# Two transformer blocks on one core: VectorE takes all four channel tiles of the short convolution, GpSimd none

## The chip, the cores and the metric

The kernel runs on one core of a Trainium2 chip, as one launch. The metric is the device time of one execution in microseconds. The difference between two kernels is told as the ratio of their times on the same chip.

## The reference

Two blocks of two layers each work on one sequence of 256 tokens with 2048 channels, all in float32. The change touches the convolution mixer of the first block's two layers. Both layers multiply x by `w_in` (2048 x 7168), cut the product into ten parts, run three mixers (convolution, gated recurrence "hgrn2", retention) on them, multiply by `w_out`, and end with a feed-forward part. The convolution mixer is:

```python
def conv_mixer(a_in, gate_in, w_dw, b_dw, ln_g, ln_b):      # 512 channels, width 31, causal
    u = a_in * jax.nn.sigmoid(gate_in)
    y = lax.conv_general_dilated(u, w_dw[:, None, :], window_strides=(1,),
                                 padding=[(CONV_WIDTH - 1, 0)],
                                 dimension_numbers=('NWC', 'WIO', 'NWC'),
                                 feature_group_count=D_CONV) + b_dw
    return jax.nn.silu(layer_norm(y, ln_g, ln_b))
```

Each channel has its own 31 weights: for 512 channels and 256 tokens, output t of a channel is the sum over 31 taps of weight times the input at t - 30 + tap, plus a bias. The second block (attention and a delta rule) is not touched.

## The kernel before

**Weights.** All large products stream their weights from memory in blocks of 256 rows by 512 columns. SyncE loads a block into one of eight buffers `raw`, ScalarE makes its high half `w_hi` (`act_split`, L229), VectorE the low half `w_lo` = raw - w_hi (`dve_split`, L236), each in four slots, and TensorE runs twelve matmuls per block (`pe_block`, L252 to L254: hi by hi, hi by lo, lo by hi, for two row tiles and two token tiles). Semaphores tie the steps: SyncE reloads a buffer when VectorE has done its split (`lo_ready`), ScalarE may convert block c + 4 when TensorE has finished block c (`block_done`), VectorE follows ScalarE (`hi_ready`), TensorE waits for `lo_ready` (L245). Eight blocks make a unit of 512 output columns, which ScalarE copies out of the accumulators (L344).

**Mixers beside the weights.** After the first two units (the convolution's columns), the remaining twelve units of `w_in` run interleaved with the mixers. Each engine's program is written out by hand with an object `Meanwhile`, called `run`: `run(n)` puts the engine's part of the next n blocks between two mixer steps, `upto(run, n)` goes on to block n. ScalarE's and VectorE's parts are four blocks ahead of TensorE's.

**The convolution.** Channels lie on partitions in four tiles of 128. TensorE turns weights (L858) and gated input (L864) after four blocks; VectorE copies them to `conv_w` and `conv_u` (L887, L889), the latter with 30 zero columns ahead. In `dve_conv` VectorE goes through 31 taps. For each tap it treats the first three tiles (`DVE_CONV` = 3), one instruction each: the first tap writes y = u * w + bias (L898), every other one y = u * w_tap + y on 128 x 256 elements (L901), after waiting (`conv_tap`) for the instruction that made the same tile's y at the tap before. Then comes one split, `run(1)`, and, after taps 22, 26 and 27, steps of the recurrence's forget gate (`dve_hgrn_gates`: L1088 and L1089 read the turned gate out of the accumulators; L1098; L1100; in layer 1 also L1103 to L1111). Each tap is thus paired with one weight block.

**GpSimd's tile.** The fourth tile is GpSimd's (`pool_conv`, L839 to L850). [...] It starts when the first VectorE tap has signalled. After it GpSimd's next work waits for `h_cum` from VectorE (L1048).

**What waits for the convolution.** TensorE turns the forget gate after block 26 (L937), then goes on to block 38 (42 in layer 1), waits for all VectorE taps and for GpSimd's last (L872, L873), and turns the result back (L876) for the layer norm. ScalarE, after 28 blocks, waits for L1089, and computes softplus and the like (L998 to L1006), one split among them, then goes on with splits; from L1008 it waits for L1100 (in layer 1 for L1111) before the exponential of L1010 or L1014.

These are the lines in which a tap is paired with a split:

```python
        run(1)
        dve_hgrn_gates(dve, k, l, tap)
```

Of the kernel before, what the change touches and what calls it, by code (L numbers as in the profile page):

```python
# [21 lines left out]
DEPTH = 2  # L22
# [4 lines left out]
CONV_C = 512  # L27
CONV_W = 31
# [619 lines left out]
LOG_LB_MAX = math.log(1 - 1e-6)  # L648
LOG_1M_LB_MIN = math.log(1e-6)
CONV_T = CONV_W - 1 + SEQ  # L650
DVE_CONV = CONV_C // P - 1
LATE = 4


# [8 lines left out]
def first_buffers(k):  # L663
    K = 1024
    w, t1, t2 = k.scratch, k.t1, k.t2
# [38 lines left out]
    k.r_mv = k.sb_small("r_mv", [P, TT * HEADS, 2])  # L704
    k.r_rstd = k.sb_small("r_rstd", [P, TT * HEADS])
    count = k.count
    k.conv_pool, = count("conv_pool")
    k.conv_pad, k.conv_gate, k.h_gate, k.h_qsilu, k.r_gate = count("conv_pad", "conv_gate", "h_gate", "h_qsilu", "r_gate")
    k.conv_weights, k.conv_gated, k.conv_turned, k.conv_back, k.conv_var = \
        count("conv_weights", "conv_gated", "conv_turned", "conv_back", "conv_var")  # L710
# [111 lines left out]
    a.activation(ca, ca, ACT.Silu).then_inc(*k.conv_done.up())  # L822


def pool_conv(pool, k):

    g = k.nc.gpsimd

    def step(ins):
        ins.then_inc(*k.pool_step.up())  # L830
        pool.wait_ge(*k.pool_step.now())

    def weight(n):
        return k.conv_w[:, DVE_CONV, n:n + 1].to_broadcast([P, SEQ])

    y = k.conv_y[:, DVE_CONV, :]
    pool.wait_ge(*k.conv_tap.next("pool"))
    k.conv_tap.next("pool", DVE_CONV * CONV_W - 1)
    step(g.tensor_tensor(y, k.conv_u[:, DVE_CONV, 0:SEQ], weight(0), ALU.mult))  # L839
    g.tensor_tensor(k.conv_work[:, 1, :], k.conv_u[:, DVE_CONV, 1:1 + SEQ], weight(1), ALU.mult)  # L840
    step(g.tensor_tensor(y, y, weight(CONV_W), ALU.add))
    for tap in range(1, CONV_W):

        if tap + 1 < CONV_W:
            g.tensor_tensor(k.conv_work[:, (tap + 1) % 2, :], k.conv_u[:, DVE_CONV, tap + 1:tap + 1 + SEQ], weight(tap + 1),  # L845
                            ALU.mult)
        last = g.tensor_tensor(y, y, k.conv_work[:, tap % 2, :], ALU.add)
        if tap + 1 < CONV_W:
            step(last)
    last.then_inc(*k.conv_pool.up())  # L850


def pe_conv(pe, k, l, run):

    run(4)
    pe.wait_ge(*k.conv_rows_in.next("pe", 32))
    for c in range(4):
        last = k.nc.tensor.transpose(k.ps[:, 0, c * 32:(c + 1) * 32], k.conv_rows[:, c * P:(c + 1) * P],  # L858
                                     k.ident[0:CONV_W + 1, 0:CONV_W + 1])
    last.then_inc(*k.conv_weights.up())  # L860
    pe.wait_ge(*k.conv_gated.next("pe"))
    for c in range(4):
        for t in range(TT):
            last = k.nc.tensor.transpose(k.ps[:, 1 + c // 2, (c % 2) * SEQ + t * P:(c % 2) * SEQ + (t + 1) * P],  # L864
                                         k.proj[:, t, CA + c * P:CA + (c + 1) * P], k.ident)
    last.then_inc(*k.conv_turned.up())
    run(22)
    pe.wait_ge(*k.conv_tap.next("pe", 1))
    pe_hgrn_gates(pe, k, l, run)
    upto(run, 38 + LATE * l)  # L870
    pe.wait_ge(*k.h_kx.next("pe"))
    pe.wait_ge(*k.conv_tap.next("pe", DVE_CONV * CONV_W - 1))  # L872
    pe.wait_ge(*k.conv_pool.next("pe"))  # L873
    for t in range(TT):
        for c in range(4):
            last = k.nc.tensor.transpose(k.ps[:, 1 + t, c * P:(c + 1) * P], k.conv_y[:, c, t * P:(t + 1) * P], k.ident)  # L876
    last.then_inc(*k.conv_back.up())


def dve_conv(dve, k, l, run):  # L880
# [11 lines left out]
    dve.wait_ge(*k.dve_step.now())  # L892
    sem, done = k.conv_tap.now()
    for tap in range(CONV_W):
        for c in range(DVE_CONV):
            u, y = k.conv_u[:, c, tap:tap + SEQ], k.conv_y[:, c, :]
            if tap == 0:
                ins = v.tensor_scalar(y, u, k.conv_w[:, c, 0:1], k.conv_w[:, c, CONV_W:CONV_W + 1], ALU.mult, ALU.add)  # L898
            else:
                dve.wait_ge(sem, done + DVE_CONV * (tap - 1) + c + 1)  # L900
                ins = v.scalar_tensor_tensor(y, u, k.conv_w[:, c, tap:tap + 1], y, ALU.mult, ALU.add)  # L901
            ins.then_inc(*k.conv_tap.up())
        run(1)
        dve_hgrn_gates(dve, k, l, tap)
# [5 lines left out]
    for t in range(TT):  # L910
        last = v.bn_aggr(k.conv_mv[:, t, :], k.conv_stats[:, t, :])
# [483 lines left out]
def second_buffers(k):  # L1395
    K = 1024
    w, t1 = k.scratch, k.t1
# [80 lines left out]
    count, later = k.count, k.later  # L1478
# [17 lines left out]
    k.at_y, k.dn_wT, k.dn_w_kept, k.dn_turned, k.dn_turn_kept = \  # L1496
        later(DEPTH, k.r_roped, k.r_rope_free, k.r_qT, k.r_q, k.r_kT)
    k.dn_tap, k.dn_silu, k.dn_squared = later(DEPTH, k.r_k, k.r_o, k.r_var)
    k.dn_summed, = later(DEPTH * DVE_CONV * CONV_W, k.conv_tap)
    k.dn_rooted, k.dn_scaled, k.dn_qkT = later(DEPTH * (LEVELS + 1), k.h_rel, k.h_decay, k.h_factors)  # L1500
    k.dn_qkT_kept, k.dn_abs = later(DEPTH * (LEVELS + 2), k.h_scores, k.h_score_kept)
    k.dn_soft, k.dn_lnb = later(DEPTH * HEADS, k.r_scores, k.r_kept)
# [1312 lines left out]
def two_blocks_kernel(nc, dram, out):  # L2815
    k = set_up(nc, dram, out)
# [4 lines left out]
    with nc.Block() as block:  # L2821
# [26 lines left out]
        def _(pool):  # L2848
# [6 lines left out]
            for l in range(DEPTH):  # L2855
                if l:
                    pool.wait_ge(*k.turned.next("pool", BLOCKS))
                pool_first_rows(pool, k, l)
                pool_conv(pool, k)
                pool_hgrn(pool, k)  # L2860
                pool_retention(pool, k, l)

# [171 lines left out]
```

## Time and profile before

| | |
|---|---|
| Median of the timed runs | 3781.74 us (three runs, 3781.71 to 3783.3) |
| Profiled execution, span from first to last instruction | 3784.1 us |
| TensorE matmuls busy | 3541.0 us (94%) |
| VectorE busy | 2168.7 us (57%) |
| ScalarE busy | 1618.5 us (43%) |
| GpSimd busy | 419.4 us (11%) |
| TensorE's mean granted clock | 0.968 of full |
| L901 (taps on VectorE) | 180 instructions, 112.5 us |
| L845 (products on GpSimd) | 58 instructions, 62.4 us |

No time of the profiled execution other than its span is given; the page of the profile describes that one execution, which is 2.4 us longer than the median of the timed runs. Shares of busy time are means over the whole span; the convolution lies at about 92 to 203 us (layer 0) and 1351 to 1469 us (layer 1), so its stretches are read by themselves. The names are PE for TensorE, PEld for its weight load, DVE for VectorE, ACT for ScalarE, POOL for GpSimd. L12 is line 12 of the kernel. In a timeline, a row gives start, length, engine, line, operation, tiles and count; a count over one is a merged run of like instructions; in brackets stands the idle time of the engine before it and what ended it. Lengths of neighbours overlap slightly, so distances are taken from start to start.

### The profile page before, as it was taken

How to read it: one execution, taken by the hardware profiler on the slowest of the kernel's cores; microseconds unless marked ns; L12 is line 12 of the kernel's file. 1: busy time of each engine (PE TensorE's matmuls, PEld its weight loads, DVE VectorE, ACT ScalarE, POOL GpSimd, SP SyncE). 2: the span in 40 equal slices, each digit the busy share in tenths (PEclk: the TensorE clock that was granted, in tenths of full speed). 3: DMA queues.
4: the chain of work that ended last, by engine and by line, in shares of the span. 5: the costliest groups of instructions: out<-in, count | busy, mean ns of one | idle time of the engine just before them, and what ended most of it. 6: DMA issues, size and time to landing. Idle time of an engine off the chain costs nothing.

```text
span 3784.1 us, 45287 instructions
## 1 busy us (share of the span) xinstructions
PE 3541.0 (94%) x16538; PEld 2940.2 (78%) x16538; DVE 2168.7 (57%) x2397; ACT 1618.5 (43%) x1953; POOL 419.4 (11%) x330
## 2 busy tenths in 40 slices
PE   7899989999999888989899999999999978999979
PEld 6677778887888766777788888888888777788767
DVE  4976564555555587665555545565447544645544
ACT  3444334343434335433444443444445433355543
POOL 0614000000000060140100000000000041000100
PEclk9999999999999999999999999999989889999989
DMA  6444456655565555445566666556646200565534
GB/s 224 137 150 148 163 173 186 195 185 182 185 188 184 165 151 149 134 150 187 203 190 188 192 186 192 185 187 193 194 136 175 87 6 31 165 193 169 160 104 134
DMA packets 310641, 615.57 MB, mean 163 GB/s; under 512 B 19082, under 2 KB 19113, under 8 KB 308539
## 3 DMA queue, kind: packets, MB, share of 16 engines
q1 hardware_dynamic: 306144, 591.73, 50.6%
q0 software_dynamic: 4320, 21.34, 1.8%
q8 instruction: 128, 2.10, 0.2%
q14 instruction: 49, 0.40, 0.0%
HBM read 610.90 MB, written 2.10 MB: 162 GB/s over the span
## 4 chain that ended last, share of the span: by engine, by line
PE 81%; DVE 13%; ACT 4%; issue 2%; DMA 0%; POOL 0%; SPq 0%; DVEq 0%; ACTq 0%
PE ps_unit L252 24%; PE ps_unit L254 24%; PE ps_unit L253 24%; DVE sb_w_lo L236 4%; DVE sb_conv_y L901 2%; PE ps_mix L2324 2%; ACT sb_w_hi L229 2%; PE ps_mix L975 1%; PE ps_mix L376 1%; PE ps_mix L530 1%; DVE sb_h_s L1167 1%; PE ps_mix L1995 1%; PE ps_mix L2322 0%; DMA sb_raw<-in_w_in_dram 0%; PE ps_mix L2679 0%
## 5 line engine op out<-in xcount | busy, mean ns | idle before, releaser
L236 DVE TENSOR_TENSOR sb_w_lo<-sb_raw,sb_w_hi 128x1024 fp32r<-128x1024 f32 x1120 | 1407.7, 1264 | 1311.6 <-ACT sb_w_hi L229 1305.9
L229 ACT ACTIVATE sb_w_hi<-sb_raw 128x1024 fp32r<-128x1024 f32 x1120 | 1183.1, 1060 | 1838.1 <-PE ps_unit L254 1823.6
L252 PE MATMUL ps_unit<-sb_w_hi,sb_a_hi 128*128 128x512 f32 x3456 | 1383.1, 400 | 87.1 <-DVE sb_w_lo L236 56.0
L253 PE MATMUL ps_unit<-sb_w_lo,sb_a_hi 128*128 128x512 f32 x3456 | 1361.4, 394 | 0.0
L254 PE MATMUL ps_unit<-sb_w_hi,sb_a_lo 128*128 128x512 f32 x3456 | 1361.1, 394 | 0.0
L252 PEld LDWEIGHTS ps_unit<-sb_w_hi,sb_a_hi 128*128 128x128 f32 x3456 | 660.1, 191 | 242.9 <-DVE sb_w_lo L236 49.5
L254 PEld LDWEIGHTS ps_unit<-sb_w_hi,sb_a_lo 128*128 128x128 f32 x3456 | 658.5, 191 | 141.3
L253 PEld LDWEIGHTS ps_unit<-sb_w_lo,sb_a_hi 128*128 128x128 f32 x3456 | 660.0, 191 | 132.8
L252 PE MATMUL ps_unit<-sb_w_hi,sb_f_hi 128*128 128x512 f32 x1024 | 399.9, 391 | 0.0
L254 PE MATMUL ps_unit<-sb_w_hi,sb_f_lo 128*128 128x512 f32 x1024 | 398.6, 389 | 0.0
L253 PE MATMUL ps_unit<-sb_w_lo,sb_f_hi 128*128 128x512 f32 x1024 | 398.4, 389 | 0.0
L254 PEld LDWEIGHTS ps_unit<-sb_w_hi,sb_f_lo 128*128 128x128 f32 x1024 | 192.2, 188 | 40.3
L253 PEld LDWEIGHTS ps_unit<-sb_w_lo,sb_f_hi 128*128 128x128 f32 x1024 | 192.3, 188 | 39.5
L252 PEld LDWEIGHTS ps_unit<-sb_w_hi,sb_f_hi 128*128 128x128 f32 x1024 | 192.2, 188 | 39.3
L608 POOL TENSOR_TENSOR sb_relu<-sb_relu 128x1024 f32<-128x1024 f32 x32 | 61.9, 1934 | 1188.2 <-ACT sb_relu L590 1188.2
L901 DVE SCALAR_TENSOR_TENSOR sb_conv_y<-sb_conv_u,sb_conv_w,sb_conv_y 128x256 f32<-128x256 f32 x180 | 112.5, 678 | 0.1
L404 ACT ACTIVATE sb_a_hi<-ps_mix 128x512 fp32r<-128x512 f32 x88 | 50.4, 596 | 129.3 <-PE ps_mix L376 129.2
L416 DVE TENSOR_TENSOR sb_a_lo<-ps_mix,sb_a_hi 128x512 fp32r<-128x512 f32 x88 | 57.7, 686 | 74.5 <-ACT sb_a_hi L404 74.3
L360 DVE TENSOR_TENSOR sb_x<-sb_x,ps_unit 128x1024 f32<-128x1024 f32 (+1 forms) x48 | 58.6, 1221 | 30.5 <-PE ps_unit L254 30.5
L364 DVE BATCH_NORM_STATS2 sb_stats<-sb_x 128x6 f32<-128x512 f32 (+1 forms) x96 | 61.8, 685 | 3.0 <-DVE sb_x L360 0.3
L845 POOL TENSOR_TENSOR sb_conv_work<-sb_conv_u,sb_conv_w 128x256 f32<-128x256 f32 x58 | 62.4, 1076 | 4.6
L376 PE MATMUL ps_mix<-sb_square,sb_x 128*128 128x128 f32 x128 | 24.4, 349 | 36.9 <-DVE sb_x L467 25.6
(455 smaller groups left out, 2142.7 us busy)
## 6 DMA issues: line engine op xcount, KB each, us to landing
sb_raw<-in_w_ff_dram SPq DMA_DIRECT2D x512, 512.0 KB, 3.8
sb_raw<-in_w_in_dram SPq DMA_DIRECT2D x224, 512.0 KB, 3.8
sb_raw<-in_e_w_in_dram SPq DMA_DIRECT2D x112, 512.0 KB, 3.6
sb_raw<-in_o_w_in_dram SPq DMA_DIRECT2D x112, 512.0 KB, 3.7
sb_raw<-in_w_out_dram SPq DMA_DIRECT2D x64, 512.0 KB, 4.4
sb_raw<-in_e_w_out_dram SPq DMA_DIRECT2D x32, 512.0 KB, 4.4
sb_raw<-in_o_w_out_dram SPq DMA_DIRECT2D x32, 512.0 KB, 4.7
sb_raw<-in_e_w_mem_kv_dram SPq DMA_DIRECT2D x16, 512.0 KB, 4.5
```

What stands on the lines that cost most here:

```text
L229: k.nc.scalar.activation(k.w_hi[:, slot], k.raw[:, j], ACT.Copy).then_inc(k.hi_ready, 1)
L236: k.nc.vector.tensor_tensor(k.w_lo[:, slot], k.raw[:, j], k.w_hi[:, slot].bitcast(F32), ALU.subtract).then_inc(k.lo_ready, 1)
L252: k.nc.tensor.matmul(acc, hi[:, kt, tokens], w_hi, start=kt == 0, stop=False)
L253: k.nc.tensor.matmul(acc, hi[:, kt, tokens], w_lo, start=False, stop=False)
L254: last = k.nc.tensor.matmul(acc, lo[:, kt, tokens], w_hi, start=False, stop=kt == KT - 1)
L360: k.nc.vector.tensor_tensor(k.x[:, :, cols], k.x[:, :, cols], k.ps_unit[:, u % 2], ALU.add).then_inc(k.evacuated, BLOCKS)
L364: last = k.nc.vector.bn_stats(k.stats[:, t, bass.ds(chunk, 1), :].rearrange("p c s -> p (c s)"), k.x[:, t, cols])
L376: last = k.nc.tensor.transpose(bank[:, n, t * P:(t + 1) * P], tile(KB * g + n, t), k.ident)
L608: k.nc.gpsimd.tensor_tensor(k.relu2[:, u % 2], k.relu[:, u % 2], k.relu[:, u % 2], ALU.mult).then_inc(k.relu2_ready, 1)
L845: g.tensor_tensor(k.conv_work[:, (tap + 1) % 2, :], k.conv_u[:, DVE_CONV, tap + 1:tap + 1 + SEQ], weight(tap + 1), ALU.mult)
L901: ins = v.scalar_tensor_tensor(y, u, k.conv_w[:, c, tap:tap + 1], y, ALU.mult, ALU.add)
L2324: last = tensor.matmul(out[:, x, :], left[:, n, :], right[:, n, :], start=True, stop=True)
```

## The change

VectorE does each tap for four tiles, `pool_conv` and its buffer and semaphore go, and the counts on `conv_tap` are raised from three to four per tap. TensorE waits for 4 x 31 taps and for nothing of GpSimd. The rest of the kernel is as it was.

```diff
--- before.py
+++ after.py
@@ -648,7 +648,7 @@
 LOG_LB_MAX = math.log(1 - 1e-6)
 LOG_1M_LB_MIN = math.log(1e-6)
 CONV_T = CONV_W - 1 + SEQ
-DVE_CONV = CONV_C // P - 1
+CONV_TILES = CONV_C // P
 LATE = 4
 
 
@@ -669,7 +669,6 @@
     k.conv_shift = k.sb("conv_shift", t1 + 4 * K, [P, CONV_C])
     k.conv_u = k.sb("conv_u", t1 + 6 * K, [P, CONV_C // P, CONV_T])
     k.conv_y = k.sb("conv_y", t1 + 11 * K, [P, CONV_C // P, SEQ])
-    k.conv_work = k.sb("conv_work", t1, [P, 2, SEQ])
     k.conv_w = k.sb("conv_w", t1 + 15 * K, [P, CONV_C // P, CONV_W + 1])
 
 
@@ -704,7 +703,6 @@
     k.r_mv = k.sb_small("r_mv", [P, TT * HEADS, 2])
     k.r_rstd = k.sb_small("r_rstd", [P, TT * HEADS])
     count = k.count
-    k.conv_pool, = count("conv_pool")
     k.conv_pad, k.conv_gate, k.h_gate, k.h_qsilu, k.r_gate = count("conv_pad", "conv_gate", "h_gate", "h_qsilu", "r_gate")
     k.conv_weights, k.conv_gated, k.conv_turned, k.conv_back, k.conv_var = \
         count("conv_weights", "conv_gated", "conv_turned", "conv_back", "conv_var")
@@ -820,34 +818,6 @@
     act.wait_ge(*k.conv_linear.next("act"))
     ca = k.proj[:, :, CA:CA + CONV_C]
     a.activation(ca, ca, ACT.Silu).then_inc(*k.conv_done.up())
-
-
-def pool_conv(pool, k):
-
-    g = k.nc.gpsimd
-
-    def step(ins):
-        ins.then_inc(*k.pool_step.up())
-        pool.wait_ge(*k.pool_step.now())
-
-    def weight(n):
-        return k.conv_w[:, DVE_CONV, n:n + 1].to_broadcast([P, SEQ])
-
-    y = k.conv_y[:, DVE_CONV, :]
-    pool.wait_ge(*k.conv_tap.next("pool"))
-    k.conv_tap.next("pool", DVE_CONV * CONV_W - 1)
-    step(g.tensor_tensor(y, k.conv_u[:, DVE_CONV, 0:SEQ], weight(0), ALU.mult))
-    g.tensor_tensor(k.conv_work[:, 1, :], k.conv_u[:, DVE_CONV, 1:1 + SEQ], weight(1), ALU.mult)
-    step(g.tensor_tensor(y, y, weight(CONV_W), ALU.add))
-    for tap in range(1, CONV_W):
-
-        if tap + 1 < CONV_W:
-            g.tensor_tensor(k.conv_work[:, (tap + 1) % 2, :], k.conv_u[:, DVE_CONV, tap + 1:tap + 1 + SEQ], weight(tap + 1),
-                            ALU.mult)
-        last = g.tensor_tensor(y, y, k.conv_work[:, tap % 2, :], ALU.add)
-        if tap + 1 < CONV_W:
-            step(last)
-    last.then_inc(*k.conv_pool.up())
 
 
 def pe_conv(pe, k, l, run):
@@ -869,8 +839,7 @@
     pe_hgrn_gates(pe, k, l, run)
     upto(run, 38 + LATE * l)
     pe.wait_ge(*k.h_kx.next("pe"))
-    pe.wait_ge(*k.conv_tap.next("pe", DVE_CONV * CONV_W - 1))
-    pe.wait_ge(*k.conv_pool.next("pe"))
+    pe.wait_ge(*k.conv_tap.next("pe", CONV_TILES * CONV_W - 1))
     for t in range(TT):
         for c in range(4):
             last = k.nc.tensor.transpose(k.ps[:, 1 + t, c * P:(c + 1) * P], k.conv_y[:, c, t * P:(t + 1) * P], k.ident)
@@ -892,12 +861,12 @@
     dve.wait_ge(*k.dve_step.now())
     sem, done = k.conv_tap.now()
     for tap in range(CONV_W):
-        for c in range(DVE_CONV):
+        for c in range(CONV_TILES):
             u, y = k.conv_u[:, c, tap:tap + SEQ], k.conv_y[:, c, :]
             if tap == 0:
                 ins = v.tensor_scalar(y, u, k.conv_w[:, c, 0:1], k.conv_w[:, c, CONV_W:CONV_W + 1], ALU.mult, ALU.add)
             else:
-                dve.wait_ge(sem, done + DVE_CONV * (tap - 1) + c + 1)
+                dve.wait_ge(sem, done + CONV_TILES * (tap - 1) + c + 1)
                 ins = v.scalar_tensor_tensor(y, u, k.conv_w[:, c, tap:tap + 1], y, ALU.mult, ALU.add)
             ins.then_inc(*k.conv_tap.up())
         run(1)
@@ -1496,7 +1465,7 @@
     k.at_y, k.dn_wT, k.dn_w_kept, k.dn_turned, k.dn_turn_kept = \
         later(DEPTH, k.r_roped, k.r_rope_free, k.r_qT, k.r_q, k.r_kT)
     k.dn_tap, k.dn_silu, k.dn_squared = later(DEPTH, k.r_k, k.r_o, k.r_var)
-    k.dn_summed, = later(DEPTH * DVE_CONV * CONV_W, k.conv_tap)
+    k.dn_summed, = later(DEPTH * CONV_TILES * CONV_W, k.conv_tap)
     k.dn_rooted, k.dn_scaled, k.dn_qkT = later(DEPTH * (LEVELS + 1), k.h_rel, k.h_decay, k.h_factors)
     k.dn_qkT_kept, k.dn_abs = later(DEPTH * (LEVELS + 2), k.h_scores, k.h_score_kept)
     k.dn_soft, k.dn_lnb = later(DEPTH * HEADS, k.r_scores, k.r_kept)
@@ -2856,7 +2825,6 @@
                 if l:
                     pool.wait_ge(*k.turned.next("pool", BLOCKS))
                 pool_first_rows(pool, k, l)
-                pool_conv(pool, k)
                 pool_hgrn(pool, k)
                 pool_retention(pool, k, l)
```

## Rows read from the trace of the kernel before

**Rows 1.** the page: shares of the chain that ended last, by engine

```profile
PE 81%; DVE 13%; ACT 4%; issue 2%; DMA 0%; POOL 0%; SPq 0%; DVEq 0%; ACTq 0%
```

**Rows 2.** TensorE's waits, 97:160, then 1355:1420 (us, times, longest us)

```profile
PE ps_unit L252 <- DVE sb_w_lo L236: 12.8, 13, 1.1
...
PE ps_unit L252 <- DVE sb_w_lo L236: 12.4, 12, 1.1
```

**Rows 3.** windows: length, then PE, PEld, DVE, ACT, POOL, clock, DMA share, GB/s

```profile
120.00:130.00 10.00, 7.53 (x30) 5.58 (x31) 10.00 (x11) 3.53 (x4) 9.61 (x11) 1.00 0.40 110
160.00:170.00 10.00, 10.00 (x52) 8.42 (x51) 10.00 (x18) 3.66 (x4) 0.00 (x0) 1.00 0.75 213
```

**Rows 4.** VectorE's timeline beside GpSimd and alone (start us, length us, engine, line)

```profile
148.72 2.47 DVE L901 SCALAR_TENSOR_TENSOR sb_conv_y<-sb_conv_u,sb_conv_w,sb_conv_y 128x256 f32<-128x256 f32 x3
151.11 1.75 DVE L236 TENSOR_TENSOR sb_w_lo<-sb_raw,sb_w_hi 128x1024 fp32r<-128x1024 f32 x1
152.78 2.59 DVE L901 SCALAR_TENSOR_TENSOR sb_conv_y<-sb_conv_u,sb_conv_w,sb_conv_y 128x256 f32<-128x256 f32 x3
...
157.62 1.21 DVE L236 TENSOR_TENSOR sb_w_lo<-sb_raw,sb_w_hi 128x1024 fp32r<-128x1024 f32 x1
158.75 1.27 DVE L901 SCALAR_TENSOR_TENSOR sb_conv_y<-sb_conv_u,sb_conv_w,sb_conv_y 128x256 f32<-128x256 f32 x3
159.94 1.21 DVE L236 TENSOR_TENSOR sb_w_lo<-sb_raw,sb_w_hi 128x1024 fp32r<-128x1024 f32 x1
```

**Rows 5.** GpSimd's timeline, its last two convolution additions, layer 0

```profile
153.29 1.80 POOL L847 TENSOR_TENSOR sb_conv_y<-sb_conv_y,sb_conv_work 128x256 f32<-128x256 f32 x2
```

**Rows 6.** ScalarE's timeline, weight splits, layer 0, then layer 1

```profile
91.38 1.06 ACT L229 ACTIVATE sb_w_hi<-sb_raw 128x1024 fp32r<-128x1024 f32 x1 [1.66 <-PE ps_unit L254]
...
166.52 1.06 ACT L229 ACTIVATE sb_w_hi<-sb_raw 128x1024 fp32r<-128x1024 f32 x1 [3.02 <-PE ps_unit L254]
169.24 1.06 ACT L229 ACTIVATE sb_w_hi<-sb_raw 128x1024 fp32r<-128x1024 f32 x1 [1.66 <-PE ps_unit L254]
...
1350.45 1.06 ACT L229 ACTIVATE sb_w_hi<-sb_raw 128x1024 fp32r<-128x1024 f32 x1 [1.66 <-PE ps_unit L254]
...
1425.49 1.06 ACT L229 ACTIVATE sb_w_hi<-sb_raw 128x1024 fp32r<-128x1024 f32 x1 [3.62 <-PE ps_unit L254]
1428.21 1.06 ACT L229 ACTIVATE sb_w_hi<-sb_raw 128x1024 fp32r<-128x1024 f32 x1 [1.66 <-PE ps_unit L254]
```

**Rows 7.** VectorE's timeline, the first tap, layer 0, then layer 1

```profile
92.41 1.95 DVE L898 TENSOR_SCALAR sb_conv_y<-sb_conv_u,sb_conv_w 128x256 f32<-128x256 f32 x3
...
1351.49 1.36 DVE L898 TENSOR_SCALAR sb_conv_y<-sb_conv_u,sb_conv_w 128x256 f32<-128x256 f32 x3
1352.77 1.21 DVE L236 TENSOR_TENSOR sb_w_lo<-sb_raw,sb_w_hi 128x1024 fp32r<-128x1024 f32 x1
```

**Rows 8.** VectorE's timeline, gate step and starved split, layer 0, then layer 1

```profile
172.69 1.76 DVE L1088 TENSOR_SCALAR sb_h_lf<-ps_mix 128x1536 f32<-128x1536 f32 x1
...
185.28 1.23 DVE L236 TENSOR_TENSOR sb_w_lo<-sb_raw,sb_w_hi 128x1024 fp32r<-128x1024 f32 x1 [4.13 <-ACT sb_w_hi L229]
...
1431.52 1.75 DVE L1088 TENSOR_SCALAR sb_h_lf<-ps_mix 128x1536 f32<-128x1536 f32 x1
...
1447.22 1.23 DVE L236 TENSOR_TENSOR sb_w_lo<-sb_raw,sb_w_hi 128x1024 fp32r<-128x1024 f32 x1 [7.27 <-ACT sb_w_hi L229]
```

**Rows 9.** TensorE's timeline, layer 0: the starved block, the transposes of L876

```profile
186.56 0.80 PE L252 MATMUL ps_unit<-sb_w_hi,sb_a_hi 128*128 128x512 f32 x1 [3.45 <-DVE sb_w_lo L236]
...
203.03 1.03 PE L876 MATMUL ps_mix<-sb_square,sb_conv_y 128*128 128x128 f32 x8
```

**Rows 10.** ScalarE's timeline, layer 1: the table load of L1014

```profile
1461.50 1.28 ACT L1014 ACT_TABLE_LOAD   x1 [7.25 <-DVE sb_h_lf L1111]
```

**Rows 11.** TensorE alone, windows (length, busy (x), granted clock, DMA share, GB/s)

```profile
186.50:192.00 5.50, 5.44 (x13) 0.50 0.63 183
...
1475.00:1480.00 5.00, 4.76 (x14) 0.66 0.72 211
```

## The prediction

> **What bounds the kernel now.** I read the page's chain first: TensorE holds 81% of it, so time is won only where TensorE stops waiting [rows 1]. TensorE's waits in the two convolution stretches come next: 13 and 12 waits of at most 1.1 us, all for the low half of a weight block, the VectorE subtraction of L236 [rows 2]. The windows say why it is late: at 120 to 130 us VectorE is busy for all of 10 us, GpSimd for 9.61, TensorE for only 7.53; at 160 to 170 us GpSimd is silent, VectorE gets through 18 instructions instead of 11, and TensorE is full again [rows 3].
>
> VectorE's timeline gives prices as start-to-start distances. Beside GpSimd one split costs 152.78 - 151.11 = 1.67 us and three taps 151.11 - 148.72 = 2.39 (0.797 each): a period of 4.06. Alone, the split costs 1.13 and three taps 1.19 (0.397 each): 2.32 [rows 4]. The change of price comes as GpSimd's last additions end at 153.29 + 1.80 = 155.09 us [rows 5], with the same shapes and neighbours on VectorE. A VectorE busy with taps and splits is the bound until then; after it, TensorE's 2.72 us per block is.
>
> **What the change removes and adds.** GpSimd's 62 tensor operations per layer go, with its semaphore steps and TensorE's separate wait for them (now in the VectorE count). GpSimd issues no DMA there, and its next work waits for h_cum from VectorE, far later, so its saved time is worth nothing by itself. VectorE gets 62 instructions: one more per tap, 31 taps in each layer. Interleaving deepens from three to four tiles, so the wait for the tap before stays covered. All other waits, queues and block counts stay.
>
> **Price of the fourth tap.** The trace has no four-tile period. Bounds: 0.397 us per tap, GpSimd silent [rows 4], and 0.797 beside GpSimd. I take 0.397, since GpSimd is silent all through the stretch afterwards. Then a period is 1.13 + 4 x 0.397 = 2.72 us. ScalarE's split, released by TensorE, recurs every 1.66 idle + 1.06 = 2.72 us when TensorE is not held up [rows 6]. So VectorE has just TensorE's pace: it neither falls behind nor catches up. The first tap costs (1352.77 - 1351.49)/3 = 0.427 each, 1.71 for four [rows 7].
>
> A lag is allowed. ScalarE converts block c+4 when TensorE has finished block c; TensorE needs it three blocks (8.16 us) later; 1.06 + 1.13 go for the work, so VectorE may start about 5.9 us after ScalarE ends. It starts at 92.41 + 1.71 = 94.12, and ScalarE ended at 91.38 + 1.06 = 92.44: lag 1.68 [rows 6, 7]. The waits of [rows 2] go entirely.
>
> **Up to the gates (tap 22).** ScalarE's splits from 91.38 to 169.24 are 23, 22 intervals; unhindered they take 22 x 2.72 = 59.8, plus 1.36 for TensorE's turning of the forget gate (the idle time of 3.02 instead of 1.66 at 166.52): 61.2 [rows 6]. They take 77.86 now. **Gain 16.66.** In layer 1 the same count runs from 1350.45 to 1428.21, 77.76, against 59.84 + 1.96 (3.62 - 1.66): **gain 15.96** [rows 6]. That is more than the waits add up to (12.8, 12.4) because each wait also breaks TensorE's overlap of one matmul with the next.
>
> **Gates and last taps, layer 0.** From here I count from ScalarE's split at 169.24, call it T. During TensorE's turning VectorE makes up 1.36 of its lag, leaving 0.32. It starts the gate step L1088 at T + 1.06 + 0.32 + 1.13 = T + 2.5; now it is 172.69 = T + 3.45 [rows 8]. The chain from there runs through ScalarE's exponentials and logarithms to the split at 185.28, 12.59 later, and does not shorten; TensorE starves behind it for 3.45 us [rows 8, 9]. That wait ends 0.95 earlier. Then VectorE has taps 25 to 30 left, with the added tap each: 6 x 0.397 = +2.38, and TensorE, which needs the last tap for the transposes of L876, waits for it. Check by VectorE's total: 1.71 + 30 x 1.59 + 31 x 1.135 + 6.8 for the gate instructions (L1088, L1089, L1098, L1100, all of L1088's size, about 1.7 each) + 3.9 idle in ScalarE's chain (4.13 now) = 95.2 us after 92.41. T is then 91.38 + 61.2 = 152.6, so the last tap ends at T + 35.0 and the transposes start at T + 35.1, against 203.03 = T + 33.8 now [rows 9]. **Given back 1.3.** So the wait to watch is a new one, about 2 us of TensorE's, at L876.
>
> **Layer 1.** The turning (1.96) exceeds the lag, so L1088 starts at T + 2.3 instead of 1431.52 = T + 3.3; the starved split, now 1447.22, comes 1.0 earlier [rows 8]. Taps 25 to 27 add 1.2 before ScalarE's L1014, which waits 7.25 us for VectorE's L1111 [rows 10]: net +0.2. Behind it ScalarE's long chain sets the pace, TensorE turns the convolution only after block 42, and taps 28 to 30 lie beside that chain. **Given back 0.2.**
>
> **Sum:** 16.66 - 1.3 + 15.96 - 0.2 = 31.1 us less. Nothing later waits by absolute time: the weight loads are released by the splits, with eight buffers, and the stages behind the convolution move along with TensorE. The profiled span is 3784.1, 2.4 above the median of 3781.7 of the timed runs; as the sum is a difference I take it from the median: **3750.6 us**.
>
> **A rule against it.** In both stretches VectorE is busy without a gap [rows 3]. The Trainium skill, Perfetto Trace Analysis, on balancing work across engines, says that when VectorE is saturated, moving work to ScalarE or even GpSimd may make sense, which read alone is against this change; it adds that between VectorE and GpSimd it might not help, since they share a read port. By the first half, with the price beside GpSimd kept, the sum would be rival A's; by the second it is mine. SBUF — State Buffer, section on who interferes with whom, names the condition: a VectorE instruction with two SBUF inputs against a GpSimd instruction that reads SBUF. The pair of prices, 0.797 and 0.397, agrees with the second half.
>
> **Rivals.**
> A. *VectorE becomes the bound (slower).* If a tap kept 0.797 and a split 1.67, a period would be 4.86 against 4.06: 23 taps add 18 us before the gates, the last 8 taps another 3 to 6, so 22 us per layer: about 3826. It decides from the period at which the first 23 taps take as long as now, (172.69 - 92.41)/23 = 3.49 us: a tap of 0.59. For it: VectorE is full. Against: [rows 4] show 0.397 in this kernel, on this data, beside the same ScalarE and DMA work, and one row is after GpSimd's end, not a mean. Chance 0.03.
> B. *The gain is partly eaten by new stalls and a low clock.* TensorE's granted clock is 0.50 (1.2 of 2.4 GHz) after the 3.45 us starvation and 0.66 in the window after 1475 us, where short waits precede it [rows 11]. From 186.5 to 192.0 it runs at half pace, and half of those 5.5 us is lost: 2.7. The new wait at L876 could bring one such spell in layer 0, and another phase of waits one in layer 1; if moreover VectorE's period is 2.78 instead of 2.72, the lag at the gates is 1.3 larger in each layer. Together 2 x (2.7 + 1.3) = 8: about 3758.6. Chance 0.17.
> C. *More than forecast.* The starvations at the gates get shorter (3.45 to 2.5), which could spare the low-clock spell, and the L876 wait could be smaller if a tap in four costs a little less than in three. Up to 5 us: 3746. Chance 0.10.
> D. *No difference.* TensorE's stalls would have to come from something else than VectorE's pace, such as the raw loads, which the waits of [rows 2] don't name. About 3781. Chance 0.02.
>
> **How the numbers follow.** My forecast has 0.68. The unknown tap price moves it little while VectorE stays inside its lag: at 0.42 instead of 0.397 the lag grows by 2.0, still inside 5.9, and 2 to 3 us per layer come back at the gates. The range takes in B and C with about 2 us beyond each, 3744 to 3760; A and D, 0.05, lie outside, and I leave some 0.1 for a mis-sized term. A measurement of this kernel can tell about 0.2% (7.6 us) from no change; my case, B and C all lie beyond that. Faster 0.94, same 0.03 (D and the far end of B), slower 0.03 (A).
>
> **What would show it.** L901: 240 instructions, close to 0.48 us mean duration by form everywhere, period split plus four taps 2.72 us. L236 in the stretch at 1.22 instead of 1.76. TensorE's many 1.1 us waits gone in both layers; its starved waits at the gates about 1 us shorter in each layer (3.45 to 2.5 in the first); a wait of about 2 us for L901 ahead of L876 in layer 0. The last tap of layer 0 at 187.6 us. GpSimd silent from 92.9 to 155.1 us, where it now works 9.61 of each 10, and its wait for h_cum longer by as much. I am wrong if the taps stay over 0.5 us with GpSimd silent, or if TensorE's short waits survive under a released VectorE.

## The result and the profile after

| | before | changed |
|---|---|---|
| Median, first comparison | 3781.72 us (4 runs) | 3741.69 us (4 runs, 3738.22 to 3743.44) |
| Ratio, 95% interval | | 0.9896 [0.9882, 0.991] |
| Median of all executions timed in this study | 3780.2 us (51) | 3742.3 us (14) |
| Span of the first profiled execution | 3784.1 us | 3736.4 us |

The changed kernel is faster by 40.0 us in the first comparison, and by 37.9 over all executions (95% by resampling them: 35.2 to 40.9). The forecast was a gain of 31.1 us, to 3750.6, with 3744 as the lower end of the range: the direction was right, the gain was put too small, and the measured time lies outside the range.

The page of the changed kernel, four lines that answer to those of before (its taps are L870 now):

```profile
span 3736.4 us, 45225 instructions
PE 3519.9 (94%) x16538; PEld 2933.0 (78%) x16538; DVE 2138.6 (57%) x2459; ACT 1618.0 (43%) x1953; POOL 300.8 (8%) x206
...
PE 83%; DVE 10%; ACT 4%; issue 2%; DMA 1%; POOL 0%; SPq 0%; DVEq 0%; ACTq 0%; POOLq 0%
...
L236 DVE TENSOR_TENSOR sb_w_lo<-sb_raw,sb_w_hi 128x1024 fp32r<-128x1024 f32 x1120 | 1391.3, 1249 | 1295.1 <-ACT sb_w_hi L229 1289.3
...
L870 DVE SCALAR_TENSOR_TENSOR sb_conv_y<-sb_conv_u,sb_conv_w,sb_conv_y 128x256 f32<-128x256 f32 x240 | 100.1, 481 | 0.1
```

VectorE's taps are 240 instead of 180 and still cost less, 100.1 against 112.5 us, since one takes 0.48 instead of 0.68 us. TensorE's waits from 97 to 205 us (layer 0), then from 1320 to 1445 us (layer 1), both wider than the stretches of [rows 2] (us, times, longest), and the window from 120 to 130 us, whose columns are those of [rows 3]:

```profile
PE ps_unit L252 <- DVE sb_w_lo L236: 3.9, 2, 2.6
PE ps_mix L845 <- DVE sb_conv_y L870: 1.4, 1, 1.4
...
PE ps_unit L252 <- DVE sb_w_lo L236: 10.6, 3, 5.7
```

```profile
120.00:130.00 10.00, 10.00 (x46) 8.29 (x45) 10.00 (x20) 4.28 (x6) 0.00 (x0) 1.00 0.62 182
```

The 13 and 12 waits of [rows 2] are gone. Three kinds are left: the starvation at the gates (2.6 and 5.7), waits after it, and the new wait for the last tap at L845 (the L876 of before). VectorE is as full as before, 10.00 of 10, with 20 instructions in place of 11, and TensorE is full beside it. VectorE's timeline, in the stretch, at the gate step, and the splits behind the last tap:

```profile
128.03 1.68 DVE L870 SCALAR_TENSOR_TENSOR sb_conv_y<-sb_conv_u,sb_conv_w,sb_conv_y 128x256 f32<-128x256 f32 x4
129.61 1.23 DVE L236 TENSOR_TENSOR sb_w_lo<-sb_raw,sb_w_hi 128x1024 fp32r<-128x1024 f32 x1
130.75 1.68 DVE L870 SCALAR_TENSOR_TENSOR sb_conv_y<-sb_conv_u,sb_conv_w,sb_conv_y 128x256 f32<-128x256 f32 x4
...
155.26 1.75 DVE L1057 TENSOR_SCALAR sb_h_lf<-ps_mix 128x1536 f32<-128x1536 f32 x1
...
187.61 3.50 DVE L236 TENSOR_TENSOR sb_w_lo<-sb_raw,sb_w_hi 128x1024 fp32r<-128x1024 f32 x3
```

Four taps take 129.61 - 128.03 = 1.58 us, a split 1.14: 2.72 together, as [rows 4] promised. ScalarE's splits that bound the counted intervals, layer 0 (the one at 150.30 has the idle time of 3.02 for TensorE's turning, as in [rows 6]), then layer 1:

```profile
91.81 1.06 ACT L229 ACTIVATE sb_w_hi<-sb_raw 128x1024 fp32r<-128x1024 f32 x1 [1.66 <-PE ps_unit L254]
...
150.30 1.06 ACT L229 ACTIVATE sb_w_hi<-sb_raw 128x1024 fp32r<-128x1024 f32 x1 [3.02 <-PE ps_unit L254]
153.02 1.06 ACT L229 ACTIVATE sb_w_hi<-sb_raw 128x1024 fp32r<-128x1024 f32 x1 [1.66 <-PE ps_unit L254]
...
1323.79 1.06 ACT L229 ACTIVATE sb_w_hi<-sb_raw 128x1024 fp32r<-128x1024 f32 x1 [1.66 <-PE ps_unit L254]
...
1385.59 1.06 ACT L229 ACTIVATE sb_w_hi<-sb_raw 128x1024 fp32r<-128x1024 f32 x1 [1.66 <-PE ps_unit L254]
```

From 91.81 to 153.02 are 61.21 us, against 77.86 before, and from 1323.79 to 1385.59 are 61.80 us, against 77.76. TensorE at the starved block, at the transposes, and at two waits of layer 1:

```profile
169.11 0.80 PE L252 MATMUL ps_unit<-sb_w_hi,sb_a_hi 128*128 128x512 f32 x1 [2.59 <-DVE sb_w_lo L236]
...
187.85 1.06 PE L845 MATMUL ps_mix<-sb_square,sb_conv_y 128*128 128x128 f32 x8 [1.38 <-DVE sb_conv_y L870]
...
1421.68 0.76 PE L252 MATMUL ps_unit<-sb_w_hi,sb_a_hi 128*128 128x512 f32 x1 [3.86 <-DVE sb_w_lo L236]
...
1432.73 0.47 PE L252 MATMUL ps_unit<-sb_w_hi,sb_a_hi 128*128 128x512 f32 x1 [0.99 <-DVE sb_w_lo L236]
```

### The profile page after: what moved, and what is told of

Read it like the earlier page. It is cut to its first block, busy times and chain, and to the rows that moved or that the text cites. A ratio compares the mean times of both kernels' runs of the same rounds, so it can differ in the third digit from the quotient of the medians.

```text
span 3736.4 us, 45225 instructions
## 1 busy us (share of the span) xinstructions
PE 3519.9 (94%) x16538; PEld 2933.0 (78%) x16538; DVE 2138.6 (57%) x2459; ACT 1618.0 (43%) x1953; POOL 300.8 (8%) x206
## 4 chain that ended last, share of the span: by engine, by line
PE 83%; DVE 10%; ACT 4%; issue 2%; DMA 1%; POOL 0%; SPq 0%; DVEq 0%; ACTq 0%; POOLq 0%
PE ps_unit L252 25%; PE ps_unit L254 25%; PE ps_unit L253 25%; DVE sb_w_lo L236 3%; PE ps_mix L2293 2%; ACT sb_w_hi L229 2%; PE ps_mix L944 1%; PE ps_mix L376 1%; PE ps_mix L530 1%; DVE sb_h_s L1136 1%; PE ps_mix L1964 1%; PE ps_mix L2291 0%; DVE sb_conv_y L870 0%; DMA sb_raw<-in_w_in_dram 0%; PE ps_mix L2648 0%
## 5 line engine op out<-in xcount | busy, mean ns | idle before, releaser
L236 DVE TENSOR_TENSOR sb_w_lo<-sb_raw,sb_w_hi 128x1024 fp32r<-128x1024 f32 x1120 | 1391.3, 1249 | 1295.1 <-ACT sb_w_hi L229 1289.3
L870 DVE SCALAR_TENSOR_TENSOR sb_conv_y<-sb_conv_u,sb_conv_w,sb_conv_y 128x256 f32<-128x256 f32 x240 | 100.1, 481 | 0.1
L364 DVE BATCH_NORM_STATS2 sb_stats<-sb_x 128x6 f32<-128x512 f32 (+1 forms) x96 | 61.7, 685 | 3.0 <-DVE sb_x L360 0.3
L2401 DVE TENSOR_TENSOR sb_dn_rows_t<-sb_dn_rows_t,ps_mix 128x512 f32<-128x512 f32 x36 | 24.8, 689 | 59.2 <-PE ps_mix L2293 59.1
```

Of the source, the lines that this page charges most:

```text
L236: k.nc.vector.tensor_tensor(k.w_lo[:, slot], k.raw[:, j], k.w_hi[:, slot].bitcast(F32), ALU.subtract).then_inc(k.lo_ready, 1)
L364: last = k.nc.vector.bn_stats(k.stats[:, t, bass.ds(chunk, 1), :].rearrange("p c s -> p (c s)"), k.x[:, t, cols])
```

## The experiments

To place the gain, each profile is divided at three events in each layer: VectorE's first tap; ScalarE's absolute value that opens the forget gate (L998 before); and VectorE's statistics of the turned convolution (L908 before). The last column ends at the statistics of the last layer norm (L364). Lengths in us, start to start:

| kernel | layer 0: first tap to gate | gate to statistics | to layer 1's first tap | layer 1: first tap to gate | gate to statistics | from there to the last statistics |
|---|---|---|---|---|---|---|
| before, two profiles | 83.74, 83.73 | 33.01, 33.02 | 1142.3, 1138.9 | 83.48, 83.47 | 53.54, 53.55 | 2291.2, 2291.3 |
| changed, three profiles | 65.86, 65.85, 65.86 | 35.30, 35.29, 35.29 | 1130.8, 1131.0, 1130.8 | 66.45, 66.44, 66.45 | 53.12, 53.10, 53.10 | 2287.7, 2284.9, 2288.4 |
| three tiles, GpSimd idle | 65.86 | 32.91 | 1134.0 | 66.45 | 53.52 | 2291.3 |
| four tiles beside GpSimd's work | 92.30 | 35.23 | 1135.6 | 92.20 | 54.71 | 2288.4 |
| four tiles beside GpSimd's memsets | 66.31 | 35.24 | 1137.1 | 66.45 | 53.12 | 2284.6 |
| a fifth operation | 74.99 | 37.25 | 1131.6 | 74.85 | 54.31 | 2281.2 |
| splits between the tables | 65.85 | 33.68 | 1132.7 | 66.45 | 49.72 | 2288.3 |
| the same, turn two blocks later, two profiles | 65.85, 65.85 | 37.59, 37.64 | 1133.2, 1132.0 | 66.45, 66.45 | 49.74, 49.74 | 2284.3, 2288.0 |

Line numbers shift from kernel to kernel: the taps are L901 before, L870 changed, and L902, L893 or L872 in the runs. "The stretches" below are the four columns of the two layers. They repeat to some hundredths of a us; the two other columns, where the programs are the same, do not.

**The two kernels again.** No edit. Three runs, for the size and for further profiles.

> The changed kernel once more, to size the effect and get a second profile. Open: the medians lie 40 us apart where the ledger of the two convolution stretches gives 31, and the two profiles show 31.6 in those stretches and about 16 outside them. Theory P (the excess lies outside the stretches, in spells of low TensorE clock that fall differently): the ratio stays 0.988 to 0.991, the stretch from ScalarE's first split beside the taps to the transposes of the convolution keeps its length to 0.5 us in this second profile, and the stretches around the layer norms differ from the first profile by 1 to 5 us. Rival Q (the excess is made in the convolution stretches): those stretches differ from profile to profile.

Measured: 3743.97 us against 3778.85, ratio 0.9904 [0.9888, 0.9921].

> The kernel before once more, with a profile, for the 5 us by which the change gains more than the ledger of the two stretches. Theory P (the excess is not made in the stretches; two executions of one kernel differ by as much in when TensorE's clock falls elsewhere): the second profile has the same lengths in both convolution stretches to 0.5 us (77.9 and 77.8 us for 22 intervals of ScalarE's splits), a span several us below 3784, and the difference lies in the turns and layer norms. Rival Q: the stretches themselves differ.

Measured: 3781.06 against 3779.17 for its partner, ratio 1.0004 [0.9993, 1.0014]; the gap between two sets of the same kernel is 2 us.

> The changed kernel a third time, for the size alone. The two stretches are shorter by 33.0 us by the profiles (15.6 and 17.4), a ratio of 0.9913 by themselves. If nothing outside them differs but by chance: a median 33 us below that of the kernel before, give or take 3. If TensorE's clock is systematically better elsewhere in the changed kernel: 38 to 40 us again, and the parts outside the stretches some 8 us shorter in this profile too.

Measured: 3742.46 against 3781.84, ratio 0.9904 [0.9888, 0.9921]. The stretches add up to 253.8 us before and 220.7 changed: 33.0 us less, every time. The medians of this comparison lie 39.4 us apart, within the 38 to 40 that the second reading named, and 33.0 lies below the 95% interval over all executions, 35.2 to 40.9. So the rest is not chance alone, and it lies outside the stretches. Rival Q fell; what is known of the outside part stands further below.

**GpSimd gone, nothing added to VectorE.** This kernel leaves out 30 of the 31 taps of the fourth tile.

```diff
-                pool_conv(pool, k)
-    pe.wait_ge(*k.conv_pool.next("pe"))
+    v.tensor_scalar(k.conv_y[:, DVE_CONV, :], k.conv_u[:, DVE_CONV, 0:SEQ], k.conv_w[:, DVE_CONV, 0:1],
+                    k.conv_w[:, DVE_CONV, CONV_W:CONV_W + 1], ALU.mult, ALU.add)
     for tap in range(CONV_W):
         for c in range(DVE_CONV):
```

> Leaves out part of the computation: VectorE does three tiles as in the kernel before, the fourth tile gets its first tap only, GpSimd nothing. So GpSimd's load is gone and VectorE has no added work. Theory (VectorE was slowed by GpSimd, and the added taps lie beside TensorE's pace up to the gates): VectorE's taps at 0.40 us, the 22 intervals of ScalarE's splits 61.2 and 61.8 us as in the changed kernel, and only the last taps shorter, 6 x 0.40 us in layer 0: 1 to 3 us below the changed kernel. Rival (the added taps cost their own time, 62 x 0.40 = 25 us): 20 us or more below the changed kernel, near 3717.

Measured: 3743.31 us, ratio 0.9909 [0.9893, 0.9924]. VectorE's timeline:

```profile
111.82 1.27 DVE L902 SCALAR_TENSOR_TENSOR sb_conv_y<-sb_conv_u,sb_conv_w,sb_conv_y 128x256 f32<-128x256 f32 x3
113.40 1.23 DVE L236 TENSOR_TENSOR sb_w_lo<-sb_raw,sb_w_hi 128x1024 fp32r<-128x1024 f32 x1 [0.31 <-ACT sb_w_hi L229]
114.54 1.27 DVE L902 SCALAR_TENSOR_TENSOR sb_conv_y<-sb_conv_u,sb_conv_w,sb_conv_y 128x256 f32<-128x256 f32 x3
```

The taps are at 0.40 us, and the split now waits 0.31 us for ScalarE: VectorE has to spare what a fourth tap takes. The way to the gate is as long as with four tiles (65.86, 66.45); the added taps show only behind it, 35.30 - 32.91 = 2.4 us in layer 0 and nothing in layer 1. So the whole gain is GpSimd's silence, and by the stretches the added instructions cost 2.0 of the 25 us that they last (218.7 against 220.7 us). The medians, 3743.3 and 3742.3, are too coarse to show that.

**Four tiles, with GpSimd's operations kept.** GpSimd's function of before stays, with a buffer of its own as the sum:

```diff
-    y = k.conv_y[:, DVE_CONV, :]
+    y = k.conv_dummy[:]
```

> VectorE does all four tiles, and GpSimd does its 62 tensor operations a layer all the same, on the same inputs, into a buffer that nobody reads (conv_y and conv_w lie 512 bytes lower for it). Theory (two SBUF inputs on VectorE against GpSimd's reads): a tap costs 0.80 and a split 1.67 us while GpSimd works, a period 4.86 us, for some 13 periods; TensorE stalls again by some 2 us per block; per layer 22 to 28 us over the changed kernel: 3785 to 3800, slower than before or equal. Rival (the price beside GpSimd comes from the interleaving of three tiles or from the DMA traffic, not from GpSimd): taps at 0.40 us, 3742 as the changed kernel.

Measured: 3798.34 us, ratio 1.0054 [1.0038, 1.0069]: slower than before. VectorE's timeline:

```profile
110.27 1.63 DVE L236 TENSOR_TENSOR sb_w_lo<-sb_raw,sb_w_hi 128x1024 fp32r<-128x1024 f32 x1
111.82 3.32 DVE L902 SCALAR_TENSOR_TENSOR sb_conv_y<-sb_conv_u,sb_conv_w,sb_conv_y 128x256 f32<-128x256 f32 x4
115.07 1.75 DVE L236 TENSOR_TENSOR sb_w_lo<-sb_raw,sb_w_hi 128x1024 fp32r<-128x1024 f32 x1
116.74 3.35 DVE L902 SCALAR_TENSOR_TENSOR sb_conv_y<-sb_conv_u,sb_conv_w,sb_conv_y 128x256 f32<-128x256 f32 x4
```

Four taps now take 115.07 - 111.82 = 3.25 us, 0.81 each, a split 116.74 - 115.07 = 1.67, the period is 4.92. The windows, while GpSimd works and after:

```profile
120.00:130.00 10.00, 7.55 (x24) 5.26 (x24) 10.00 (x12) 2.38 (x3) 9.61 (x11) 0.83 0.36 107
160.00:170.00 10.00, 10.00 (x49) 8.14 (x48) 10.00 (x19) 4.58 (x5) 0.00 (x0) 1.00 0.61 197
```

The price follows GpSimd's activity within one kernel and between two kernels with one VectorE program. The stretches are 53.7 us longer than in the changed kernel.

The counts in the windows say in what form the price is paid. VectorE and GpSimd start 12 and 11 instructions in this window, and 11 and 11 in that of the kernel before [rows 3]; over all of GpSimd's work on layer 0, from its fourth operation to its last, the trace has 59 of its operations beside 59 of VectorE's instructions, in both kernels. This is what one would see if each VectorE instruction waited for one GpSimd operation, long or short as it may be: 0.797 - 0.397 = 0.40 us more for a tap of 256 elements, 1.67 - 1.13 = 0.54 for a split of 1024. Over a period of before this is (4.06 - 2.32)/4 = 0.44 us per instruction, with the fourth tap (4.92 - 2.72)/5 = 0.44 again. How much of a GpSimd operation this is can't be told, as no run times GpSimd's operations without VectorE.

A thing not asked for: the granted clock is 0.83 in the first window, although no wait of TensorE in this stretch is over 1.9 us long.

**Four tiles, GpSimd only writing.**

```diff
+    for tap in range(WRITES):
+        g.memset(k.conv_work[:, tap % 2, :], 0.0)
+        last = g.memset(k.conv_dummy[:], 0.0)
```

> As the run with four tiles beside GpSimd, but GpSimd runs 124 memsets of 128x256 a layer in place of its tensor operations: it writes SBUF and reads nothing. Theory R (only GpSimd's reads contend with VectorE's second input): taps stay at 0.40 us and splits at 1.22 us beside the memsets, time within 3 us of the changed kernel. Rival W (any GpSimd instruction holds VectorE up): taps near 0.8 us and over 3770. This run also shows what the shift of the two buffers by 512 bytes is worth: nothing, by both.

Measured: 3742.25 us, ratio 0.9906 [0.9891, 0.9921]. Groups by form from 104 to 150 us, VectorE, then GpSimd, and the window from 120 to 130 us:

```profile
L893 DVE SCALAR_TENSOR_TENSOR sb_conv_y<-sb_conv_u,sb_conv_w,sb_conv_y 128x256 f32<-128x256 f32 x69 | 28.7, 474 | 0.0
L236 DVE TENSOR_TENSOR sb_w_lo<-sb_raw,sb_w_hi 128x1024 fp32r<-128x1024 f32 x17 | 20.6, 1213 | 0.0
...
L838 POOL MEMSET sb_conv_work<- 128x256 f32 x44 | 13.7, 312 | 2.5
```

```profile
120.00:130.00 10.00, 10.00 (x45) 8.29 (x45) 10.00 (x20) 4.28 (x5) 9.08 (x33) 1.00 0.62 181
```

Taps take 474 ns and splits 1213, as alone. The memsets end at 131.0 us, before the end of the stretch that these means cover, so the price is read from the part beside them: four taps take 121.21 - 119.63 = 1.58 us, 0.395 each, while memsets fill 9.08 of 10 us:

```profile
119.63 1.66 DVE L893 SCALAR_TENSOR_TENSOR sb_conv_y<-sb_conv_u,sb_conv_w,sb_conv_y 128x256 f32<-128x256 f32 x4
121.21 1.21 DVE L236 TENSOR_TENSOR sb_w_lo<-sb_raw,sb_w_hi 128x1024 fp32r<-128x1024 f32 x1
```

A write-only load does not hold VectorE up; GpSimd's reading tensor operations do. By the Trainium skill, SBUF — State Buffer, the section on who interferes with whom, this is the rule: a VectorE instruction with two SBUF inputs contends with a GpSimd instruction that reads SBUF, not with one that only writes. The two runs agree with it, 0.81 against 0.40 us. The Trainium skill, in the same page's summary of rules for kernel authors, adds that the second one to issue "fully blocks" until the first has finished. The counts of one instruction to one operation fit that. On this reading a tap's price doubles because its own 0.40 us are about as long as what it waits for, and a split's rises only by half.

**One instruction more per tap.**

```diff
+        v.scalar_tensor_tensor(k.conv_dummy[:], k.conv_u[:, last, tap:tap + SEQ], k.conv_w[:, last, tap:tap + 1],
+                               k.conv_u[:, last, 0:SEQ], ALU.mult, ALU.add).then_inc(*k.conv_extra.up())
         run(1)
```

> The changed kernel with a fifth VectorE instruction of a tap's size after each tap (its result is read by nobody, conv_y and conv_w lie 512 bytes lower). Theory (VectorE was added work exactly up to TensorE's pace; beyond it every 0.40 us counts): period 3.12 instead of 2.72 us, a slack of 4.2 us used up after some 10 blocks, then waits of TensorE of about 0.4 us at each block; 22 x 0.40 - 4.2 = 4.6 us before the gates and 8 x 0.40 = 3.2 behind them in layer 0, where also the slack is missing at the gates: 8 to 12 us per layer, 3758 to 3766. Rival (VectorE has room to spare, and the fourth tap could have been followed by a fifth for nothing): within 3 us of the changed kernel.

Measured: 3759.37 us, ratio 0.9951 [0.9933, 0.9969], 17 us over the changed kernel; its stretches are 20.7 us longer.

```profile
112.81 1.68 DVE L872 SCALAR_TENSOR_TENSOR sb_conv_y<-sb_conv_u,sb_conv_w,sb_conv_y 128x256 f32<-128x256 f32 x4
114.39 0.49 DVE L876 SCALAR_TENSOR_TENSOR sb_conv_dummy<-sb_conv_u,sb_conv_w 128x256 f32<-128x256 f32 x1
114.78 1.23 DVE L236 TENSOR_TENSOR sb_w_lo<-sb_raw,sb_w_hi 128x1024 fp32r<-128x1024 f32 x1
115.92 1.67 DVE L872 SCALAR_TENSOR_TENSOR sb_conv_y<-sb_conv_u,sb_conv_w,sb_conv_y 128x256 f32<-128x256 f32 x4
```

The period is 115.92 - 112.81 = 3.11 us. The gate comes 9.1 us later in layer 0, the full 23 x 0.40, where 4.6 us had been expected: it stands in VectorE's own order, and TensorE's slack does not help it. The fourth tap filled VectorE to TensorE's pace, and the fifth is paid for.

**The table loads of the gate.** In ScalarE's gate step one split more:

```diff
     step(a.activation(k.h_d1[:], k.h_d1[:], ACT.Exp, scale=-1.0))
+    run(1)
     a.activation(k.h_d1[:], k.h_d1[:], ACT.Ln, bias=1.0).then_inc(*k.h_softplus.up())
     if l:
         act.wait_ge(*k.h_lb_log.next("act"))
+        run(1)
```

> The changed kernel, with one more weight split of ScalarE between the exponential and the logarithm of the forget gate, and in layer 1 one more ahead of the small logarithms; the order of the splits is the same, only the gate's steps come later between them. Theory (TensorE starves at the gates because ScalarE's table loads and activations hold back the split of one block): the waits of 2.6 and 5.7 us go or fall under 1 us with the low clock behind them, VectorE loses its idle time of some 4 us, and as VectorE's taps bind in layer 0 the gain there is 3 to 4 us; in layer 1 ScalarE's later chain binds, gain 1 to 4 us: 3733 to 3739. Rival (the gate's chain to VectorE's L1067 is what TensorE really waits for, and is now longer): no gain, the waits move behind tap 26.

Measured: 3738.16 us, ratio 0.9889 [0.9872, 0.9905]. ScalarE's timeline, then TensorE's waits, layer 0 and layer 1:

```profile
163.12 1.49 ACT L969 ACTIVATE sb_h_d<-sb_h_d 128x1536 f32<-128x1536 f32 x1
164.64 1.06 ACT L229 ACTIVATE sb_w_hi<-sb_raw 128x1024 fp32r<-128x1024 f32 x1
165.72 1.28 ACT L971 ACT_TABLE_LOAD   x1
```

```profile
PE ps_unit L252 <- DVE sb_w_lo L236: 3.5, 3, 1.5
PE ps_mix L845 <- DVE sb_conv_y L870: 1.4, 1, 1.4
...
PE ps_unit L252 <- DVE sb_w_lo L236: 8.1, 5, 3.9
```

The stretches are 5.0 us shorter than in the changed kernel. The starvation of 2.6 us has become three waits of at most 1.5, as VectorE's chain binds behind it, and layer 0 gains 1.6 us, where 3 to 4 had been expected. In layer 1 8.1 of 10.6 us of waits stay, the longest of 3.9 behind VectorE's L1111, and the gain is 3.4, within the 1 to 4. The waits did not fall under 1 us as expected. The median is 4.1 us below that of the changed kernel, but with 5 and 14 executions whose times overlap that could be chance (95%: -0.8 to 10.5).

**The turn of the convolution two blocks later in layer 0**, on top of that:

```diff
-    upto(run, 38 + LATE * l)
+    upto(run, 38 + late_of(l))
...
+def late_of(l):
+    return LATE if l else 2
```

> As the run with the splits between the tables, and in layer 0 TensorE turns the convolution two blocks later (40 instead of 38), with all later mixer steps of that layer moved along by two blocks on every engine. Theory: the wait of 1.4 us of TensorE for the last tap goes, worth 1 to 2 us on top of the run before: 3731 to 3738. Rival: the steps moved by two blocks collide with something later (the rest of the units is fixed, so the retention steps come nearer to the end): 0 to 5 us slower than without the move.

Measured: 3738.31 us, ratio 0.9886 [0.9868, 0.9903]: no gain over the run before in the median, and just above the forecast's upper end.

> The kernel with the splits between the tables and the convolution's turn two blocks later, once more beside the changed kernel. By the profiles its stretches are 5.0 (tables) and 1.5 us (the wait for the last tap) shorter than the changed kernel's: a median 4 to 8 us below it. If the steps moved by two blocks cost something later: less than 4.

Measured: 3737.82 us, ratio 0.9886 [0.9867, 0.9905], beside 3742.46 for the changed kernel: 4.6 us less. The wait for the last tap is gone; less the two blocks (2 x 2.72) that now lie ahead of the statistics, the part from gate to statistics is 37.6 - 5.4 = 32.2 instead of 33.7 us. In the medians these 1.5 us don't show. All four executions (3736.68 to 3738.63) lie below all five of the changed kernel (3739.01 to 3747.12), so this variant is faster; for the one without the move the medians alone don't show it. Which of the two is better isn't told by these runs.

## Why the prediction was right and wrong

**Right: what bound the kernel.** The prices of [rows 4], 0.797 and 0.397, belong to GpSimd's reading operations (runs with GpSimd's work kept and with memsets), and VectorE with four tiles has exactly TensorE's 2.72 us. Rival A, the price kept, was made real in part by the run with GpSimd's operations kept, for as long as they last: some 50 of the 124 taps of a layer start beside them. Its stretches are 53.7 us over the changed kernel's, and it ends 56 above it (3798.3 - 3742.3) and 20 above its partner of before, where A, with the price kept for all taps, had been given 44 (3826 - 3782). It is no outcome of the change itself.

**Right: the ledger of layer 0.** The 22 intervals of ScalarE's splits gained 77.86 - 61.21 = 16.65 us, forecast 16.66. That this is more than the 12.8 us of waits was put down to TensorE's broken overlap of matmuls; the size came out, that reason was not tested by itself. From tap to gate 17.9 us less were measured, forecast were 16.66 + 0.95 = 17.6. The last tap was forecast to end 95.2 us after the first began: the splits behind it begin 187.61 - 92.85 = 94.8 us after it. The wait at the transposes was forecast at about 2 and is 1.4, the starved one at 2.5 and is 2.6. Gate to statistics costs 2.3 more, forecast 0.95 + 1.3 = 2.25. Rival B's low clock behind the new wait did not come: the window from 190 to 200 us has a granted clock of 1.00. Rival C's shorter spell did come: behind the starved block the clock was 0.69 from 169.0 to 174.5 us, where [rows 11] has 0.50. It paid nothing, since the length came out as forecast without it.

**Right: layer 1 up to the gate:** 17.0 us, forecast 15.96 + 1.0.

**Wrong, 1.6 us: "Given back 0.2" in layer 1.** From gate to statistics 1.0 + 0.2 us more were forecast, and 0.4 less were measured. Up to the last wait of TensorE (it ends at 1475.24 before, 1432.73 changed) the part is 1.2 us longer, as forecast; behind it, it is 11.7 instead of 13.3 us. I carried on the waits of before as they stood, with their clock. Before, TensorE waited 1.9 us at 1475 us and then ran in a window at 0.66 of its clock [rows 11]; now the wait there is 0.99 us and the next blocks run at full clock, while the spell of low clock lies behind the wait of 3.86 us at 1421.68, where TensorE has to wait for ScalarE's chain again and the lost time is hidden. TensorE alone (length, busy (x), granted clock, DMA share, GB/s), the changed kernel:

```profile
1420.00:1430.00 10.00, 8.32 (x30) 0.83 0.43 121
1430.00:1440.00 10.00, 9.01 (x44) 1.00 0.68 236
```

So a spell moved from work that counts to work that waits.

**Wrong, some 5 us: "the stages behind the convolution move along with TensorE".** The sum put the rest of the kernel at nothing. The stretches explain 33.0 of the 37.9 us between the medians; 4.9 are made where both programs are the same. The profiles overstate that part, 11 to 17 us: the three profiled executions of the changed kernel were 3 to 8 us shorter than the medians of their sets, the two of the kernel before 2 to 4 longer. So the table's columns outside the stretches show places, not the size.

Two places behind layer 1's convolution are the same in every profile. From VectorE's statistics of the retention (L1339 before) to those of the next layer norm (L364) are 47.4 us before and 45.9 to 46.0 changed; and between two layer norms' statistics further on (the last at 1929.4 us before, 1884.4 changed) are 133.0 and 130.6 to 130.7 us. At the first, TensorE alone (length, busy (x), granted clock, DMA share, GB/s), the kernel before (its second profile), then the changed one, each in windows from the same point of the work:

```profile
1703.00:1706.00 3.00, 3.00 (x9) 0.50 0.00 0
1706.00:1709.00 3.00, 3.00 (x11) 0.58 0.00 0
1709.00:1712.00 3.00, 3.00 (x17) 1.00 0.00 0
```

```profile
1661.80:1664.80 3.00, 3.00 (x10) 0.62 0.00 0
1664.80:1667.80 3.00, 3.00 (x17) 1.00 0.00 0
1667.80:1670.80 3.00, 3.00 (x17) 1.00 0.00 0
```

In the first, TensorE's clock is 0.58 in the second window and full from the third on; in the other it is full from the second on, and 17 instead of 11 matmuls start in it. The longer lengths stand in all three profiles of kernels with three tiles on VectorE (47.4 and 133.0 also with GpSimd idle), the shorter ones in all nine with four tiles, even beside GpSimd's work (45.9 and 130.7), although their stretches differ by up to 59 us. So neither GpSimd nor the absolute moment decides it, and these 1.5 + 2.3 = 3.8 us may be most of the 4.9. That they are is not shown, and why the clock meets the programs differently there stays open.

Other places take one of two lengths without such an order: the part from the layer norm's statistics (L364) at some 882 us to those at some 1000 us is 115.8, 118.8 and 115.3 us long in the three profiles of the changed kernel. The whole part between the layers took 1130.8 to 1142.3 us over all kernels. In the medians the outside part is shorter than before's for each of the other kernels too, by 2 to 8 us (median of all executions of before, 3780.2, less the run's median, less the difference of the stretches, with the two blocks taken off where the turn is later), so the excess is not the changed kernel's alone.

**The range.** 3744 rested on bounds of the prices and on rival C, which named the low clock only at the gates. The failed step is thus a term put at nothing, the outside part, with 4.9 us, and a mis-sized one, 1.6 us in layer 1; the gain in the stretches, 33.0 us, alone would have given 3748.7, inside the range. With up to 8 us from outside the stretches below rival C's 3746 it should have reached down to 3738. B and D did not happen.

## What to carry to other kernels

Before work is split between VectorE and GpSimd, read VectorE's price of one instruction with GpSimd at work and silent: here one fourth of the taps on GpSimd made the other three fourths, and the splits beside them, twice and one and a half times as dear, so that taking it back cost VectorE less than nothing. Count VectorE's instructions and not only their lengths: each paid 0.40 to 0.54 us, so short ones suffer most for their length. The room for added work is the pace of the engine that sets the end (2.72 us per block) less what the engine does in it at the undisturbed price; inside it four taps were free, beyond it every one counts. A ledger from start-to-start distances holds to tenths of a us for the stretches that it covers; what happens in the rest, though both programs are the same there, was worth 2 to 8 us in 3780 and belongs in the range.

## What the runs showed of the hardware that was not expected

- TensorE's granted clock fell to 0.83 over 10 us in the run with four tiles beside GpSimd, with no wait over 1.9 us in that stretch; with the waits of at most 1.1 us of the kernel before it stayed at 1.00 in the same window [rows 3].
- Beside GpSimd's reading tensor operations VectorE and GpSimd advanced one for one, 59 instructions to 59, and each VectorE instruction took 0.40 (256 elements) to 0.54 us (1024 elements) longer.
- The same program part took 1130.8 to 1131.0 us in three profiles of one kernel and 1138.9 to 1142.3 in two of another, while the stretches beside it repeated to some hundredths of a us.
- One VectorE program has two prices by what GpSimd does beside it: 0.81 us a tap with tensor operations that fill 9.61 of 10 us, 0.40 us with memsets that fill 9.08.
